# The first block's attention by pairs of heads, layer one's splits on GpSimd, and the weight stream in order of use

## The chip, the cores and the metric

The kernel is one program on one core of a Trainium2 chip. Its time is the device time of a run in microseconds; several runs are given by their median. A profiled execution shows the work of each engine: TensorE (PE, with its weight loads as PEld), VectorE (DVE), ScalarE (ACT), GpSimd (POOL) and SyncE (SP), which only issues the transfers of the weights.

## The reference

Two blocks of two layers each work on 256 tokens of width 1024 in float32. The change touches the first one, a latent transformer with a context of 256 further tokens. Of its layer:

```python
mod = silu_c @ w_ada[l] + b_ada[l]                    # adaLN: 6 x 1024 columns a layer, for latent and context
h = modulate(rms_norm(x, norm1_g[l]), sh1, sc1)       # h * (1 + scale) + shift
qa, ka, va, qb, kb, vb, ga, gb = split_in_proj(h @ w_in[l])
ya = window_attention_latent(rope(qa), rope(ka), va, kac, vac, sink_a[l])  # window of 128, a sink per head
yb = full_attention_latent(rope(qb), rope(kb), vb, kbc, vbc)
x = x + gt1 * merge_branches(ya, yb, ga, gb, w_proj_a[l], w_proj_b[l], w_out[l])
x = x + gt2 * swiglu(modulate(rms_norm(x, norm2_g[l]), sh2, sc2), w_ffn_gate[l], w_ffn_up[l], w_ffn_down[l])
```

Both attentions have 8 query heads of 64 dimensions on 2 key/value heads. In the first layer the context goes the same way (512 tokens in all; context queries see only the 256 context keys), in the second only the latent tokens are updated. The second block (sparse attention, stick-breaking attention, an mLSTM) isn't changed.

## The kernel before

**Weights.** All weights come as one stream of 504 slots of 512 KB (eight 128x128 blocks each), which SyncE loads in order into a ring of SLOTS = 7 buffers `raw`; the load of slot n waits until slot n - 7 is released. Every projection is float32 as three fp32r products: ScalarE rounds a slot to `high` (L1141), VectorE makes `low = raw - high` (L1507), and L745 to L747 multiply high by high, high by low, low by high. `high` and `low` have PAIRS = 4 buffers; a slot is released when its `low` is made. The slots of the adaLN weights are "plain": they are used from `raw` as they are (L826), 32 columns of the stationary side (silu(c)) at a time in column group k % 4, and released when used. A chunk of 512 adaLN columns is eight such products from four slots, then `adacopy` (VectorE, PSUM to SBUF), `adac` (TensorE, L838) and `mod` (VectorE).

**Order.** A planner (`Order`, `order_of_work`) writes one list of steps by hand, and every engine walks the same list and does its part of each step, in that order, with semaphores between them. `prepare` puts the `split` steps in as early as ring and buffers allow; `pool_share` says how many of them GpSimd takes in VectorE's place: (0, 1), none, up to the end of the first block. `o.hold` keeps splits out of the norms. `fill(n)` interleaves n blocks of waiting projections (`o.filling`) with a chain of small steps.

**Start.** adaLN chunks 0, 1 and 2, with the sums of squares of x and context between them, then mean, root (GpSimd's power, L1458) and broadcast (L867), then chunk 3, and then `gs` (scale factors) and the norm's eight tiles: L1625 scales, ScalarE adds the shift (high part), L1646 makes the low part. All four chunks must be there before the first tile. The constant tables (960 and 704 KB) are asked for on ScalarE's queue behind x and context.

**Layer.** Keys (2 slots), values (2 slots), in layer one adaLN chunks 4 and 5, queries (8 slots), the head norms of the second branch with fills of 3 + 3 blocks, then the attention. Its fill is, in layer one, chunks 6 and 7 and then gate tile and chunk in turn (16 gate tiles G of eight blocks, chunks 8 to 23), in layer two the 16 gate tiles alone (half as wide). Before, a unit is one head h, one branch b (0: window and sink, 1: full) and 128 queries t; layer one has 64 units, half of them with 512 keys and half with 256, layer two 32 with 512 keys. An iteration is: scores of unit i (L904), four fill blocks, transposes of unit i - 2 (L915), values of unit i - 3 (L928). VectorE adds the window (L1683), takes the maximum (L1685) and the sink (L1690); ScalarE takes the exponential with its sum (L1261); the turned probabilities are copied by ScalarE (L1271), each fourth by VectorE (L1700). After eight units `finish` divides by the sums (L1719) and `deliver` transposes the output (L941) and copies it over the queries (L1285). The score banks are 2, 3, 4, the transposes' 5 and 6, the values collect in bank 7.

Of the kernel before, what the change touches and what calls it, by code (L numbers as in the profile page):

```python
# [6 lines left out]
P = 128  # L7
# [18 lines left out]
ADA_EARLY = 4  # L26

# [45 lines left out]
class Order:  # L73
# [3 lines left out]
    def __init__(self, plain, total):  # L77
        self.plain, self.total = plain, total
# [4 lines left out]
        self.pool_share, self.hold = (0, 1), False  # L83
        self.sweeps, self.left_at, self.block_of, self.sweep_of = 0, {}, {}, {}
        self.ada_slots, self.uncollected = {}, []
# [19 lines left out]
    def prepare(self):  # L105
        if self.hold:
            return
        while self.next_split < self.total:
            n = self.next_split
            if n not in self.plain:  # L110
# [8 lines left out]
                self.step("split", n)  # L119
                self.released.add(n)  # L120
# [5 lines left out]
    def use(self, slot):  # L126
        if slot not in self.split_no:
            self.hold = False
            self.prepare()
# [44 lines left out]
    def ada(self, c):  # L174
        for k in range(KT):
            self.ada_slots[self.at // BLK] = 4 * c + k // 2 + 1
# [20 lines left out]
def order_of_work(plain, total):  # L197
    o = Order(plain, total)
# [29 lines left out]
    def first(l):  # L228
        last = l == N_LAYERS - 1
        n = SEQ if last else ALLT  # L230
        o.pool_share = (0, 1)
# [38 lines left out]
        units = [(b, t, h) for t in range(n // P) for b in range(2) for h in range(NH)]  # L270
        per = 4
        pending = []
        for i in range(len(units) + 4):
            if i < len(units):
                o.step("S", l, i, *units[i])
            o.fill(per)
            if pending and i % 8 == 5:
                o.step("deliver", l, *pending.pop(0))
            if 2 <= i < len(units) + 2:
                o.step("turn", l, i - 2, *units[i - 2])  # L280
            if 3 <= i < len(units) + 3:
                b, t, h = units[i - 3]
                o.step("PV", l, i - 3, b, t, h)
                if h == NH - 1:
                    o.step("finish", l, b, t)
                    pending.append((b, t))
        while pending:
            o.step("deliver", l, *pending.pop(0))
# [137 lines left out]
    for chunk, tiles in enumerate((range(0, 2), range(2, 5), range(5, 8))):  # L426
        o.run(o.ada(chunk))
        for k in tiles:
# [1694 lines left out]
```

## Time and profile before

| | us |
|---|---|
| median of 3 runs | 2274.36 (2271.99 to 2285.28) |
| profiled execution | 2274.49 |
| its span, first to last instruction | 2273.0 |
| TensorE busy | 2064.7 (91%) |
| VectorE busy | 1133.1 (50%) |
| ScalarE busy | 876.5 (39%) |
| GpSimd busy | 37.2 (2%) |
| mean granted TensorE clock | 0.944 |

Busy time is the union of an engine's instructions; the ends of matmuls are modelled, so that a start-to-start distance tells more than a duration. A float32 product (L904, L928, L826, L838) leaves two records, an fp32r product and a transpose one. Times in a timeline are from the span's start. Layer one of the first block runs from about 54 to 958 us (its attention from 193 to 464), layer two up to about 1412 (attention from 1037 to 1159), the second block behind it.

### The profile page before, as it was taken

To read this page: it belongs to the slowest core of one execution; us is meant where nothing else is said; L and a number is where in the kernel's file an instruction comes from. 1 tells how busy PE (TensorE), PEld (TensorE's weight loads), DVE (VectorE), ACT (ScalarE), POOL (GpSimd) and SP (SyncE) were. 2 spreads that over 40 slices of the span, in tenths; PEclk is the share of its full clock that TensorE was granted. 3 is DMA by queue.
4 is the path that set the end of the run, shared out by engine and by line. 5 is a ranking of instruction groups with operands and counts; after the bars stand their busy time and mean duration, and the time that the engine had idled before them with its cause. 6 is when DMAs were issued, how large, how long until landed. Compare 5 with 4: busy or idle time off the path is not lost.

```text
span 2273.0 us, 30554 instructions
## 1 busy us (share of the span) xinstructions
PE 2064.7 (91%) x12588; PEld 1714.5 (75%) x12588; DVE 1133.1 (50%) x1976; ACT 876.5 (39%) x1488; POOL 37.2 (2%) x37
## 2 busy tenths in 40 slices
PE   4899999998999999899988998898997889899886
PEld 1665666676788888687778998877787888778786
DVE  2334333364433333545455655568445756764555
ACT  2212333442321222333454444455452544644442
POOL 0000000000000000000000000000000000000100
PEclk7899999989999999899998999899998989999998
DMA  8223335522222222132123564433332444232231
GB/s 315 115 91 122 139 139 186 189 89 75 83 93 86 99 94 84 64 130 75 66 75 131 191 199 173 141 123 106 117 112 76 138 139 157 85 130 105 95 110 54
DMA packets 76554, 272.26 MB, mean 120 GB/s; under 512 B 8192, under 2 KB 11392, under 8 KB 76416
## 3 DMA queue, kind: packets, MB, share of 16 engines
q1 hardware_dynamic: 72576, 264.27, 33.4%
q10 hardware_dynamic: 3840, 6.04, 0.7%
q8 instruction: 100, 1.64, 0.3%
q14 instruction: 38, 0.31, 0.0%
HBM read 269.23 MB, written 1.05 MB: 119 GB/s over the span
## 4 chain that ended last, share of the span: by engine, by line
PE 73%; DVE 14%; ACT 6%; issue 3%; DMA 2%; POOL 1%; ACTq 0%; DVEq 0%; POOLq 0%
PE bank L745 19%; PE bank L747 18%; PE bank L746 18%; DVE low L1507 4%; PE bank L904 4%; PE bank L928 3%; ACT high L1141 3%; PE bank L915 2%; PE bank L826 2%; PE bank L867 1%; DMA xc<-ctx_in 1%; PE bank L893 1%; PE bank L838 1%; POOL few L1458 1%; DVE tmp L1625 1%
## 5 line engine op out<-in xcount | busy, mean ns | idle before, releaser
L745 PE MATMUL bank<-h,high 128*128 128x256 f32 (+1 forms) x2432 | 809.8, 333 | 54.1 <-issue 10.5
L746 PE MATMUL bank<-h,high 128*128 128x256 f32 (+1 forms) x2432 | 769.0, 316 | 0.0
L747 PE MATMUL bank<-h,low 128*128 128x256 f32 (+1 forms) x2432 | 769.0, 316 | 0.0
L1507 DVE TENSOR_TENSOR low<-raw,high 128x1024 fp32r<-128x1024 f32 x408 | 496.7, 1224 | 500.8 <-ACT high L1141 500.4
L745 PEld LDWEIGHTS bank<-h,high 128*128 128x128 f32 x2432 | 474.0, 195 | 154.5 <-issue 60.9
L746 PEld LDWEIGHTS bank<-h,high 128*128 128x128 f32 x2432 | 475.2, 195 | 29.8 <-issue 2.4
L747 PEld LDWEIGHTS bank<-h,low 128*128 128x128 f32 x2432 | 474.4, 195 | 30.0
L1141 ACT ACTIVATE high<-raw 128x1024 fp32r<-128x1024 f32 x408 | 426.5, 1050 | 127.0 <-PE bank L747 107.2
L1261 ACT ACTIVATE prob<-bank,small 128x512 f32<-128x512 f32 (+1 forms) x96 | 59.2, 616 | 195.9 <-DVE small L1690 111.5
L745 PE MATMUL bank<-hid,high 128*128 128x512 f32 (+1 forms) x352 | 118.2, 336 | 0.0
L746 PE MATMUL bank<-hid,high 128*128 128x512 f32 (+1 forms) x352 | 118.2, 336 | 0.0
L747 PE MATMUL bank<-hid,low 128*128 128x512 f32 (+1 forms) x352 | 118.2, 336 | 0.0
L904 PE MATMUL bank<-K,Q 64*128 64x512 f32 (+1 forms) x192 | 94.6, 573 | 0.0
L1685 DVE TENSOR_REDUCE small<-bank 128x1 f32<-128x512 f32 (+1 forms) x96 | 57.6, 600 | 63.0 <-PE bank L904 61.9
L928 PE MATMUL bank<-V,probT 128*128 128x64 f32 x640 | 83.7, 271 | 0.3 <-ACT probT L1271 0.3
L928 PEld LDWEIGHTS bank<-V,probT 128*128 128x128 f32 x640 | 80.6, 195 | 0.8 <-ACT probT L1271 0.5
L1528 DVE SCALAR_TENSOR_TENSOR xc<-bank,mod,xc 128x256 f32<-128x256 f32 x72 | 32.6, 480 | 95.9 <-PE bank L747 95.6
L1310 ACT ACTIVATE hid<-gt 128x512 fp32r<-128x512 f32 (+1 forms) x44 | 23.1, 525 | 145.2 <-DVE gt L1534 145.2
L1227 ACT ACTIVATE sq<-xc 128x256 f32<-128x256 f32 (+1 forms) x56 | 27.6, 496 | 127.0 <-DVE xc L1528 97.0
L826 PE MATMUL bank<-raw,silu_c 128*32 128x512 f32 x384 | 64.3, 644 | 9.9 <-ACT silu_c L1128 5.3
L746 PEld LDWEIGHTS bank<-hid,high 128*128 128x128 f32 x352 | 66.1, 188 | 8.0
L747 PEld LDWEIGHTS bank<-hid,low 128*128 128x128 f32 x352 | 66.1, 188 | 8.0
(261 smaller groups left out, 2418.9 us busy)
## 6 DMA issues: line engine op xcount, KB each, us to landing
raw<-stream SPq DMA_DIRECT2D x504, 512.0 KB, 3.3
xc<-x_in ACTq DMA_DIRECT2D x1, 1024.0 KB, 16.9
xc<-ctx_in ACTq DMA_DIRECT2D x1, 1024.0 KB, 28.4
out<-xc ACTq DMA_DIRECT2D x1, 1024.0 KB, 4.8
cst<-consts ACTq DMA_DIRECT2D x1, 960.0 KB, 28.8
cst<-consts ACTq DMA_DIRECT2D x1, 704.0 KB, 22.5
ukw<-uk ACTq DMA_DIRECT2D x1, 512.0 KB, 3.2
uvw<-uv ACTq DMA_DIRECT2D x1, 512.0 KB, 4.2
```

What stands on the lines that cost most here:

```text
L745: mm(dst, wh, xh, start=start, stop=False)
L746: mm(dst, wh, xl, start=False, stop=False)
L747: return mm(dst, wl, xh, start=False, stop=stop)
L826: ins = mm(banks[b][g, :], silu_c[:, k, :], raw[:, block // BLK % SLOTS, at:at + 512], start=k < 4, stop=k >= 4)
L904: mm(banks[b][:, 0:w], Q[l][half, 4 * b_ + h % 4, t * P:(t + 1) * P], K[l][half, b_, keys], start=True, stop=True).then_inc(S["S"], 1)
L915: ins = nc.tensor.transpose(banks[b][:, s * P:(s + 1) * P], prob[l][i % 3][:, s * P:(s + 1) * P], ident)
L928: ins = mm(banks[7][:, head(h)], probT[l][i % 2][:, s * P:(s + 1) * P], V[l][:, first + s, c:c + HD], start=s == 0, stop=s == w // P - 1)
L1141: do(high[:, i % PAIRS, :], raw[:, slot % SLOTS, :], ACTF.Copy).then_inc(S["hi"], 1)
L1261: do(prob[l][i % 3][:, 0:w], banks[bank_of[step]][:, 0:w], ACTF.Exp, bias=st[:, h:h + 1], accum_out=st[:, 8 + h:9 + h]).then_inc(S["exp"], 1)
L1507: tt(low[:, i % PAIRS, :], raw[:, slot % SLOTS, :], high[:, i % PAIRS, :].bitcast(F32), ALU.subtract).then_inc(S["lo_dve"], 1)
L1528: ins = stt(out=xc[:, jj, c], in0=ps[:, c], scalar=mod[:, at, s:s + 1], in1=xc[:, jj, c], op0=ALU.mult, op1=ALU.add)
L1685: nc.vector.tensor_reduce(st[:, h:h + 1], ps[:, 0:w], AX.X, ALU.max, negate=True).then_inc(S["masked_max"], 1)
```

## The change

- **Pairs.** A step now handles heads j and j + 4 of a branch, which lie in the two halves of the partitions of one query tile: two score products into two banks, two softmaxes, eight transposes into banks 5 and 6, both heads' values.
- **Order in an iteration.** Scores of pair i; 3 fill blocks; transposes of pair i - 1, copied by ScalarE (first head) and VectorE (second head) ahead of the exponentials of pair i; the new step `even`, in which VectorE divides the probabilities by their sum (sinks added) before they are turned; 3 fill blocks; values of pair i - LAG (1 in layer one, 2 in layer two); 2 fill blocks in layer one, 1 in layer two.
- **Values.** V is now the stationary side (64 columns) and the turned probabilities stream (128 columns); the output comes out turned and is copied from bank 7 over the queries (two copies each on ScalarE and VectorE). The transposes L941 and `finish` are gone.
- **GpSimd** makes `low` for all slots up to the end of layer one; from layer two on it is VectorE as before.
- **Start.** All sums of squares first, adaLN chunk 2, mean, chunk 3, broadcast, `gs` (which needs only 2 and 3), then chunks 0 and 1, then the norm. Its tiles 0, 3 and 6 let one split step in each. Of the constants only the identity (64 KB) comes at the start; the rest is asked for on ScalarE's queue at the norm's tile 2.
- **Stream.** A draft walk of the order finds which slot each use wants; SyncE loads `stream[source[n]]`.

```diff
 Order.__init__
-        self.pool_share, self.hold = (0, 1), False
+        self.pool_share, self.hold = (1, 1), False
...
+    def take(self, chunk=None, k=0):
+        if self.draft and self.at % BLK == 0 and self.at // BLK == len(self.source):
+            self.source.append(next(self.stream_split) if chunk is None else self.stream_plain[4 * chunk + k // 2])
...
 norm_tiles
+            if k % 3 == 0 and m == ("n1", 0):
+                o.prepare(1)
...
 first
-        o.pool_share = (0, 1)
+        o.pool_share = (1, 1) if n == ALLT else (0, 1)
...
-        for i in range(len(units) + 4):
-            if i < len(units):
-                o.step("S", l, i, *units[i])
-            o.fill(per)
...
+        pairs = [(b, t, j) for t in range(n // P) for b in range(2) for j in range(4)]
+        lag = LAG[l]
+        for i in range(len(pairs) + lag):
+            if i < len(pairs):
+                o.step("S", l, i, *pairs[i])
+            o.fill(3)
+            if 1 <= i <= len(pairs):
+                o.step("turn", l, i - 1, *pairs[i - 1])
+            if i < len(pairs):
+                o.step("exp", l, i, *pairs[i])
+                o.step("even", l, i, *pairs[i])
+            o.fill(3)
+            if i >= lag:
+                b, t, j = pairs[i - lag]
+                o.step("PV", l, i - lag, b, t, j)
+                if j == 3:
+                    o.step("deliver", l, b, t)
+            o.fill(2 if l == 0 else 1)
...
 start
+    for k in range(KT):
+        norm_sums(first_norm, k)
+    o.run(o.ada(2))
     o.step("sqsum", first_norm, KT - 1)
     o.step("mean", first_norm)
+    o.run(o.ada(3))
     o.step("bcast", first_norm)
     o.collect()
     o.step("gs", 0, 0)
+    o.run(chain(o.ada(0), o.ada(1)))
+    o.collect()
...
 TensorE, scores
+                    for g, b in enumerate(bank_of[step]):
+                        if b in freed:
+                            pe.wait_ge(*freed[b])
+                        mm(banks[b][:, 0:w], Q[l][head(g), 4 * b_ + j, t * P:(t + 1) * P], K[l][head(g), b_, keys],
+                           start=True, stop=True).then_inc(S["S"], 1)
+                        freed[b] = ("exp", 2 * no[step] - 1 + g)
...
 TensorE, values
+                    pe.wait_ge("turned_act", no[step])
+                    pe.wait_ge("turned_dve", no[step])
                     for s in range(w // P):
+                        for g in range(2):
+                            c = P * b_ + HD * g
+                            ins = mm(banks[7][head(g), j * P:(j + 1) * P], V[l][:, first + s, c:c + HD],
+                                     probT[l][2 * (i % LAG[l]) + g][:, s * P:(s + 1) * P], start=s == 0, stop=s == w // P - 1)
...
 ScalarE, exp
+                    for g, b in enumerate(bank_of["S", l, i, b_, t, j]):
+                        if b_ == 0:
+                            act.wait_ge("sink_max", sinks[l, i])
+                        do(prob[l][2 * (i % 2) + g][:, 0:w], banks[b][:, 0:w], ACTF.Exp, bias=st[:, g:g + 1],
+                           accum_out=st[:, 2 + g:3 + g]).then_inc(S["exp"], 1)
...
 ScalarE, norm
+                    if step == ("norm", ("n1", 0), 2):
+                        nc.scalar.dma_start(cst[:, :], consts).then_inc(S["in_cst"], 16)
+                        nc.scalar.dma_start(cst2[:, P:], consts2[:, P:]).then_inc(S["in_cst2"], 16)
...
 VectorE, even
+                    dve.wait_ge("exp", at + 1)
+                    if b_ == 0:
+                        dve.wait_ge("sunk_exp", sinks[l, i])
+                        tt(st[:, 2:4], st[:, 2:4], st[:, 4:6], ALU.add).then_inc(S["dve_own"], 1)
+                    nc.vector.reciprocal(st[:, 6:8], st[:, 2:4]).then_inc(S["dve_own"], 1)
+                    for g in range(2):
+                        p = prob[l][2 * (i % 2) + g][:, 0:w]
+                        ts(p, p, st[:, 6 + g:7 + g], None, ALU.mult).then_inc(S["even"], 1)
...
 SyncE
-                nc.sync.dma_start(raw[:, n % SLOTS, :], stream[n]).then_inc(S[f"slot{n % SLOTS}"], 16)
+                nc.sync.dma_start(raw[:, n % SLOTS, :], stream[work.source[n]]).then_inc(S[f"slot{n % SLOTS}"], 16)
```

## Rows read from the trace of the kernel before

**Rows 1.** Table by stretch: length, busy us and instructions by engine, PE clock, DMA, GB/s
```profile
193.00:454.00 261.00, 258.14 (x1451) 173.68 (x1451) 94.63 (x203) 90.90 (x214) 0.00 (x0) 0.99 0.44 161
...
600.00:700.00 100.00, 100.00 (x430) 80.57 (x429) 34.49 (x36) 28.16 (x36) 0.00 (x0) 1.00 0.27 95
```

**Rows 2.** TensorE's timeline, 512-key unit, layer one: start us, us, engine, line
```profile
226.42 1.12 PE L904 MATMUL bank<-K,Q 64*128 64x512 f32 x2
227.47 1.07 PE L826 MATMUL bank<-raw,silu_c 128*32 128x512 f32 x8
228.47 0.66 PE L915 MATMUL bank<-cst,prob 128*128 128x128 f32 x4
228.96 1.00 PE L928 MATMUL bank<-V,probT 128*128 128x64 f32 x8
229.89 1.12 PE L904 MATMUL bank<-K,Q 64*128 64x512 f32 x2
```

**Rows 3.** TensorE's timeline, part of a 256-key unit, layer one
```profile
431.48 0.56 PE L928 MATMUL bank<-V,probT 128*128 128x64 f32 x4
431.96 0.70 PE L904 MATMUL bank<-K,Q 64*128 64x256 f32 x2
432.59 1.06 PE L826 MATMUL bank<-raw,silu_c 128*32 128x512 f32 x8
```

**Rows 4.** TensorE's timeline, second block, products of two heads
```profile
1513.54 0.71 PE L980 MATMUL bank<-dqs,x 64*128 64x256 f32 x4
1514.08 0.40 PE L981 MATMUL bank<-dqs,x 64*128 64x128 f32 x4
1514.40 0.38 PE L745 MATMUL bank<-h,high 128*128 128x256 f32 x1
...
1532.26 0.40 PE L1004 MATMUL bank<-prob,SV 128*64 128x128 f32 x4
```

**Rows 5.** Groups by line, 193 to 425 us, TensorE: xcount | busy us, mean ns
```profile
L941 PE MATMUL bank<-cst,tmp 128*128 128x128 f32 x24 | 3.9, 286 | 0.0
```

**Rows 6.** Chain that ended last: start us, us, what; three adaLN products
```profile
158.58 1.01 PE bank L826 x6
```

**Rows 7.** Timelines of GpSimd and of VectorE, where both work, second block
```profile
1693.77 2.38 POOL L1466 TENSOR_TENSOR z<-z,dqs 128x1024 f32<-128x1024 f32 x1
1693.79 3.44 DVE L1866 TENSOR_TENSOR z<-z,dqs 128x1024 f32<-128x1024 f32 x1 [6.95 <-ACT dqs L1397]
```

**Rows 8.** Groups by line and form, 1037 to 1158 us (layer two's attention), VectorE
```profile
L1685 DVE TENSOR_REDUCE small<-bank 128x1 f32<-128x512 f32 x32 | 22.1, 689 | 17.0 <-PE bank L904 16.5
L1507 DVE TENSOR_TENSOR low<-raw,high 128x1024 fp32r<-128x1024 f32 x13 | 15.9, 1225 | 27.8 <-ACT high L1141 27.8
...
L1683 DVE TENSOR_TENSOR bank<-bank,cst 128x128 f32<-128x128 f32 x16 | 4.7, 295 | 9.8 <-PE bank L904 9.6
...
L1690 DVE TENSOR_TENSOR small<-small,small_sink 128x1 f32<-128x1 f32 x16 | 2.5, 159 | 0.5
```

**Rows 9.** Groups by form, 1500 to 2110 us, VectorE: scaling of 256 probabilities
```profile
L1849 DVE TENSOR_SCALAR prob<-prob,stats 128x256 f32<-128x256 f32 x16 | 5.6, 347 | 0.0
```

**Rows 10.** TensorE's timeline, layer two: the scores of two successive units
```profile
1093.22 1.12 PE L904 MATMUL bank<-K,Q 64*128 64x512 f32 x2
...
1097.12 1.12 PE L904 MATMUL bank<-K,Q 64*128 64x512 f32 x2
```

**Rows 11.** Groups by line and form, 1037 to 1158 us, ScalarE
```profile
L1261 ACT ACTIVATE prob<-bank,small 128x512 f32<-128x512 f32 x32 | 22.0, 688 | 60.8 <-DVE small L1690 34.4 <-DVE small L1685 26.3
...
L1141 ACT ACTIVATE high<-raw 128x1024 fp32r<-128x1024 f32 x13 | 13.7, 1053 | 0.0
```

**Rows 12.** Chain that ended last, in order of time, first 100 us
```profile
1.85 28.36 DMA xc<-ctx_in
...
53.83 0.88 DVE tmp L1625 x2
...
99.50 1.84 PE bank L838 x8
```

More of the change, by code:

```diff
@@ L73, with __init__ @@
 class Order:
[L77 to L78 removed]
+    def __init__(self, plain, total, source=None):
+        self.stream_plain, self.total = sorted(plain), total
+        self.stream_split = iter(n for n in range(total) if n not in plain)
+        self.draft, self.source = source is None, source or []
+        self.plain = {n for n, s in enumerate(self.source) if s in plain}
         self.steps, self.filling = [], []
@@ L103, in reload, with prepare @@
             self.loaded += 1
-    def prepare(self):
-        if self.hold:
+    def prepare(self, most=None):
+        if self.hold and not most or self.draft:
             return
-        while self.next_split < self.total:
+        while self.next_split < self.total and most != 0:
             n = self.next_split
@@ L119, in prepare @@
                 self.step("split", n)
+                most = most and most - 1
                 self.released.add(n)
@@ L501, in psum_banks @@
             bank[s[:2]] = turn("acc")
-        elif kind in ("S", "score", "latent", "read", "centre"):
+        elif kind == "S":
+            bank[s] = (turn("lgt"), turn("lgt"))
+        elif kind == "turn":
+            bank[s] = (turn("trp"), turn("trp"))
+        elif kind in ("score", "latent", "read", "centre"):
             bank[s] = turn("lgt")
@@ new lines, in vector_program @@
+                    (_, w), st, at = keys_of(t), stat(l, i), 2 * no[step] - 1
+                    for g, b in enumerate(bank_of[step]):
+                        ps = banks[b]
+                        dve.wait_ge("S", at + g)
+                        if b_ == 0 and t < 2:
+                            o = slice((1 - t) * P, (2 - t) * P)
+                            own += 1
+                            tt(ps[:, o], ps[:, o], const("window", t * P, t * P + P), ALU.add).then_inc(S["dve_own"], 1)
+                            dve.wait_ge("dve_own", own)
+                        if no[step] > 4:
+                            dve.wait_ge("even", at + g - 8)
+                        nc.vector.tensor_reduce(st[:, g:g + 1], ps[:, 0:w], AX.X, ALU.max,
+                                                negate=True).then_inc(S["masked_max"], 1)
@@ new lines, in vector_program @@
+                    dve.wait_ge("turn", 2 * no[step])
+                    if i >= LAG[l]:
+                        dve.wait_ge("PV", 2 * no[step] - 2 * LAG[l])
+                    nc.vector.tensor_copy(probT[l][2 * (i % LAG[l]) + 1][:, 0:w], banks[bank_of[step][1]][:, 0:w]).then_inc(S["turned_dve"], 1)
+                elif kind == "deliver":
+                    l, b_, t = key
+                    dve.wait_ge("PV", 8 * no[step])
+                    for odd in range(2):
+                        src, dst = out_of(l, b_, t, 1, odd)
+                        ins = nc.vector.tensor_copy(dst, src)
+                    ins.then_inc(S["delivered_dve"], 1)
```

257 lines of the change are left out of this document (98 added, 159 removed).

## The prediction

> **What bounds the kernel now.** I first read the table of stretches for the first block. Over layer one's attention TensorE works 258.14 of 261 us at a granted 0.99, VectorE 94.63 and ScalarE 90.90; in a plain stretch behind it TensorE works all 100 us, at 430 products in 100 us, so 0.233 us for a 512-column product and 5.6 us for a weight slot of 24 [rows 1]. The reader is to see that the first block is bound by TensorE's own work: what leaves its queue shortens the run, and work on the other engines costs nothing until it is late. Then I read the timeline of a unit (one head, 128 queries). With 512 keys it spends 1.05 us on the scores (L904), 0.49 on four transposes (L915) and 0.93 on the values (L928), 2.47 in all, beside 1.00 for four adaLN products (L826) [rows 2]. With 256 keys scores take 0.63 and values 0.48 [rows 3].
>
> **Scores and values by pairs.** The pair's score products use rows 0 to 63 and 64 to 127 of TensorE and different banks. No row shows that for L904, but the second block's L980/L981 is the same shape: two heads, each a 256-column and a 128-column product, are through in 0.86 us (1513.54 to 1514.40) [rows 4], where one 256-column product alone takes 0.63 [rows 3]; one after another they would need some 1.7. So two heads run side by side at the price of one. The values now hold V (64 columns) and stream 128 queries, the heads in the two halves of the columns: in L1004 four such records start at 1532.26 and take 0.40 [rows 4], of which I read about 0.11 per pair of records plus a tail (estimate). Bounds: the full gain, or none, where the two run in turn. I take the full gain, as both shapes stand in the trace. Rule: the Trainium skill, TensorEngine Tiling (Array Packing), Key Properties, says that tiles execute in parallel but that a change of tiling mode drains the engine; the rows agree with the first half, and the sum below holds its own price for changes.
>
> At 512 keys a pair has so far 2 x (1.05 + 0.49 + 0.93) = 4.94. After: scores 1.07, eight transposes 0.93 (0.16 for the first, 0.11 for each further one, as the 0.49 divides), values 8 x 0.11 + 0.2 = 1.07, together 3.07: 1.87 less. At 256 keys: 2 x (0.63 + 0.48) = 2.22 becomes 0.65 + 0.60 = 1.25: 0.97 less. Layer one has 16 pairs of each kind: 29.9 + 15.5 = 45.4 us less. The transposes of the output (L941, 24 in 3.9 us, 0.16 each [rows 5]) go: 8 x 4 x 0.16 = 5.2.
>
> **What the new fill costs.** Four adaLN products lie on four groups of 32 columns; six records, that is three products, take 1.01 us [rows 6], as long as four [rows 2]. A chunk of eight was filled 4 + 4, and is now filled 3 + 3 + 2: three groups for two. The head norms consume three sets of eight blocks before, so that each iteration holds one chunk or one gate tile: 16 chunks x 1.0 = 16 us more. One more change of shape per iteration: 32 x 0.1 = 3 (estimate from the 0.2 us between L928's last start and L904, against 0.11 in the stream of L928). Net on TensorE in layer one: 45.4 + 5.2 - 16 - 3 = 31.6 less.
>
> **GpSimd's splits.** A 128x1024 tensor-tensor takes GpSimd 2.38 us. The VectorE operation that began beside it took 3.44 [rows 7], where the same size takes 1.22 by itself [rows 8]: it ended about 1.1 after GpSimd did, so it stood still until then. Rule: the Trainium skill, SBUF — State Buffer, SBUF: two separate sides, calls the shared pair an exclusive lock which the loser of a two-input operation waits out; the row agrees. So in layer one each VectorE operation with two SBUF inputs may wait up to 2.38. In plain stretches a split has 5.6 us per slot and four slots of lead: hidden. In the attention the split of the next gate tile (ScalarE 1.05 [rows 11], then GpSimd 2.38) runs from about 1.8 to 4.2 us of an adaLN iteration; the sink operations of the first branch (two SBUF inputs) would start at 3.2 and now wait until 4.2; VectorE's copy of the transposes is queued behind them and ends at 5.35, while TensorE wants it at 4.1: 1.25 us in four iterations (two query tiles of 512 keys, two each): 5 us. With 256 keys the sinks come before GpSimd starts. Layer one: 31.6 - 5 = 27 us less.
>
> **Layer two** has only 512-key pairs, no adaLN, and splits still on VectorE: 16 x 1.87 + 16 x 0.16 - 1.6 = 31 less for TensorE. But the starts of two units lie 3.90 us apart [rows 10], 2.47 of it attention, so four blocks are 1.4 and an iteration with seven fills would be 3.07 + 0.1 + 2.45 = 5.6 us. Now the softmax is a loop over VectorE and ScalarE. For the first branch: window and maximum twice, 2 x (0.30 + 0.69 + 0.05) = 2.1 [rows 8]; sinks twice 0.16 and a start, 0.4; the copy of the turned probabilities lies beside ScalarE's two exponentials, 2 x 0.8 (0.69 [rows 11] and 0.1 for the read of the sum, an estimate); then add, reciprocal and two scalings of 512 columns (not in the trace at that width; 0.35 at 256 [rows 9]; between that and the 0.69 of a maximum, I take 0.45), 1.4: 5.8 us from maximum to maximum, and a split of 1.22 in it on most iterations: 6.6. The second branch has no windows and sinks and stays at 5.7. The mean is 6.15 against 5.6, over 15 iterations 8 us; the last pairs have no fills left and wait for the chain, 3 us more. 31 - 11 = 20 less.
>
> **The start.** The context lands at 30.2 us [rows 12] because it shares the DMA engines with the weights. TensorE now takes only chunk 2 before the mean, so 11 slots rather than 19 are asked for by then, and the constants (1.6 MB) come later: it should land at 23. But chunks 0 and 1 stand before the first norm tile on VectorE's queue (their copies, behind 8 more slots), so the first tile, 23.6 us after the context before (53.83 [rows 12]), comes 27 after it: at 50.3, 3.5 earlier. The eight tiles then meet three GpSimd splits: each second step (L1646, two SBUF inputs) can wait, and two DMA issues stand on ScalarE's queue between tiles, with VectorE and then TensorE behind: 5.5 later. Two us are lost. Behind V, four VectorE splits each wait for a transfer and stand before the copies of chunks 4 and 5, so that L838 comes at 99.50 [rows 12]; on GpSimd they block nothing: the queries start 5 us earlier. Bounds of the start: 8 less (no blocking) to 5 more. I take 2.5 less. The merge waits 1 us for blocked subtractions. The reordered stream moves no byte less; the order of use before was the stream's order, and chunks 2 and 3 first is all that changes.
>
> **Sum.** 27 + 20 + 2.5 - 1 = 48.5 less. The profiled execution took 2274.49 us, 0.1 above the median of the three; 2274.5 - 48.5 = 2226.
>
> **Rivals.** (1) *The chain decides.* The pair's softmax, two maxima, two exponentials and two scalings in series, is late in layer one too, where VectorE also copies the adaLN sums, and the scalings cost 0.69. For it: in 512-key pairs only about 1 us is free. Against it: VectorE works 94.63 of 261 [rows 1]. Half the gain in both attentions goes: 2249. (2) *No side by side.* If the wait between the two score products, or the alternation of the two value products, makes them run in turn, 1.92 per 512-key pair and 0.98 per 256-key pair come back: 32 x 1.92 + 16 x 0.98 = 77, of which layer two hides 12 in its loop: 2226 + 65 = 2291, slower by 0.7%; rows 4 speak against it. (3) *GpSimd sets the pace, the slower side.* In layer one's plain stretches some 100 slots are split by GpSimd. If a split waits for VectorE as VectorE waits for it, 2.38 + 3.44 = 5.8 is above the 5.6 us of a slot, from where the four slots of lead run out; at 6.5 a slot it costs 100 x 0.9 = 90: 2316, slower by 1.8%. Against it: VectorE has one or two such operations per slot, mostly 0.7 us. (4) *More than forecast.* No blocking, scalings at 0.35 and layer two bound by TensorE: 5 + 8 + 5: 2208.
>
> **How the numbers follow.** The forecast has 0.55, within 2214 to 2238; (1) 0.2, (2) 0.07, (3) 0.08, (4) 0.1. The range reaches to (4) and past (1): 2204 to 2260. A measurement of this kernel tells about 1% (23 us) from no change, so faster is below 2251.6: 0.55 + 0.1 and over half of (1), 0.75; slower is (3) and the far end of (2), 0.1; the rest, 0.15, is within 1%.
>
> **What would show it.** Right: pairs of L904's successor start some 14 ns apart and the pair is over in 1.1 us; the layer-one attention is about 27 us shorter and TensorE still works over 95% of it; the one of layer two shows TensorE waiting for the scaled probabilities or the maxima, and is 20 shorter; adaLN products come in groups of six, six and four records, about 1 us each; a VectorE operation beside a GpSimd split lasts 2 to 3.4 us. Wrong: score pairs of 2.1 us (rival 2), TensorE waiting for low on GpSimd in the feed-forward stretches (rival 3), waits before the transposes in layer one (rival 1).

## The result and the profile after

The changed kernel takes 2221.87 us (median; 2219.93 to 2227.03) beside 2277.34 us for the kernel before on the same chip: a ratio of 0.9759, with a 95% interval of 0.9735 to 0.9783. It is 2.4% faster. The forecast was 2226, worked out from a kernel before of 2274.5; by medians on one chip 55 us were saved. The profiled executions last 2273.0 and 2219.1 us, and 54 us lie between them.

The lines of the changed kernel have moved: scores are L930 (before L904), transposes L943 (L915), values L961 (L928), adaLN products L852 (L826), the gathering of a chunk L864 (L838), weight products L771 to L773 (L745 to L747), GpSimd's split L1472, VectorE's L1530, ScalarE's rounding L1162. I cut both executions at the same four events: the first score pair of layer one, the first `h` after its attention (ScalarE's L1315, before L1292), and the same two of layer two. The table of stretches between them, first of the kernel after, then of the kernel before (columns as in [rows 1]: stretch, length, busy us and instructions of TensorE, its weight loads, VectorE, ScalarE, GpSimd, then the granted clock):

```profile
188.30:433.60 245.30, 234.21 (x1455) 141.05 (x1454) 122.09 (x309) 87.06 (x227) 43.23 (x19) 0.98 0.50 178
433.60:1010.40 576.80, 547.00 (x2504) 440.43 (x2504) 163.60 (x290) 174.27 (x245) 199.47 (x87) 0.97 0.26 88
1010.40:1105.80 95.40, 91.49 (x761) 71.34 (x760) 75.02 (x162) 52.42 (x124) 0.00 (x0) 1.00 0.23 78
1105.80:2219.00 1113.20, 986.43 (x7124) 906.01 (x7124) 665.74 (x1166) 512.26 (x840) 19.80 (x19) 0.93 0.37 125
```

```profile
193.10:463.00 269.90, 266.01 (x1486) 180.67 (x1486) 96.73 (x207) 93.45 (x222) 0.00 (x0) 0.97 0.44 162
463.00:1037.60 574.60, 544.26 (x2504) 440.04 (x2504) 249.64 (x370) 175.65 (x246) 7.68 (x7) 0.97 0.26 88
1037.60:1158.90 121.30, 119.39 (x777) 91.82 (x776) 54.78 (x102) 55.51 (x120) 0.00 (x0) 0.99 0.18 61
1158.90:2273.00 1114.10, 988.46 (x7124) 907.06 (x7124) 665.99 (x1166) 512.39 (x841) 19.80 (x19) 0.93 0.37 125
```

The reader is to see three things. The two attentions give 24.6 and 25.9 us, the stretch before them 4.8 (193.1 to 188.3), the stretch between them loses 2.2, and the one behind them gains 0.9: 54.0 in all. In layer one TensorE's busy time fell by 31.8 us, but it now stands idle 11.1 us instead of 3.9. In layer two it fell by 27.9, with 3.9 us idle instead of 1.9.

TensorE's timeline of a 512-key pair in layer one after the change (start us, us, engine, line; x counts records, two to a product of this precision), to be held beside [rows 2]:

```profile
226.44 1.13 PE L930 MATMUL bank<-K,Q 64*128 64x512 f32 x4
227.50 1.06 PE L852 MATMUL bank<-raw,silu_c 128*32 128x512 f32 x6
228.49 0.66 PE L943 MATMUL bank<-cst,prob 128*128 128x128 f32 x4
228.98 0.60 PE L943 MATMUL bank<-cst,tmp 128*128 128x128 f32 x4
229.51 1.06 PE L852 MATMUL bank<-raw,silu_c 128*32 128x512 f32 x6
230.50 1.09 PE L961 MATMUL bank<-probT,V 128*64 128x128 f32 x16
231.53 1.05 PE L852 MATMUL bank<-raw,silu_c 128*32 128x512 f32 x4
232.51 1.13 PE L930 MATMUL bank<-K,Q 64*128 64x512 f32 x4
```

By the distances of starts, the scores of both heads take 1.06 us (one head took 1.05), the transposes 1.02 and the values 1.03. The adaLN groups of six, six and four records take 0.99, 0.99 and 0.98 us.

Where TensorE waits in layer one's attention, by the waits of the kernel after (waited for: us, times, longest):

```profile
PE bank L930 <- ACT prob L1287: 4.3, 1, 4.3
PE bank L961 <- DVE probT L1745: 4.0, 5, 0.9
PE bank L943 <- DVE mod L1594: 2.6, 1, 2.6
```

These are the first softmax, the copies of the turned probabilities, and a wait that is put down to `mod` and has its cause in GpSimd's splits, as the part on the prediction shows.

### The profile page after: what moved, and what is told of

Same layout as the page of the kernel before. It is cut to its first block, busy times and chain, and to the rows that moved or that the text cites. A ratio compares the mean times of both kernels' runs of the same rounds, so it can differ in the third digit from the quotient of the medians.

```text
span 2219.1 us, 30747 instructions
## 1 busy us (share of the span) xinstructions
PE 2004.4 (90%) x12540; PEld 1656.4 (75%) x12540; DVE 1085.8 (49%) x2044; ACT 863.9 (39%) x1494; POOL 305.6 (14%) x149
## 3 DMA queue, kind: packets, MB, share of 16 engines
HBM read 269.23 MB, written 1.05 MB: 122 GB/s over the span
## 4 chain that ended last, share of the span: by engine, by line
PE 71%; DVE 15%; ACT 7%; issue 4%; POOL 1%; DMA 1%; ACTq 0%; DVEq 0%
PE bank L771 20%; PE bank L773 18%; PE bank L772 18%; DVE low L1530 4%; ACT high L1162 3%; PE bank L852 2%; PE bank L930 2%; PE bank L961 2%; PE bank L943 1%; PE bank L893 1%; DVE h L1671 1%; PE bank L864 1%; POOL few L1481 1%; PE bank L919 1%; DVE tmp L1648 1%
## 5 line engine op out<-in xcount | busy, mean ns | idle before, releaser
L771 PE MATMUL bank<-h,high 128*128 128x256 f32 (+1 forms) x2432 | 815.5, 335 | 59.9 <-issue 13.7
L773 PE MATMUL bank<-h,low 128*128 128x256 f32 (+1 forms) x2432 | 771.0, 317 | 0.0
L771 PEld LDWEIGHTS bank<-h,high 128*128 128x128 f32 x2432 | 477.1, 196 | 147.3 <-issue 56.8
L773 PEld LDWEIGHTS bank<-h,low 128*128 128x128 f32 x2432 | 477.0, 196 | 30.8
L1530 DVE TENSOR_TENSOR low<-raw,high 128x1024 fp32r<-128x1024 f32 x296 | 360.1, 1223 | 268.3 <-ACT high L1162 267.3
L1162 ACT ACTIVATE high<-raw 128x1024 fp32r<-128x1024 f32 x408 | 426.5, 1050 | 128.6 <-PE bank L773 117.7
L1472 POOL TENSOR_TENSOR low<-raw,high 128x1024 fp32r<-128x1024 f32 x112 | 268.5, 2402 | 559.6 <-ACT high L1162 559.6
L1481 POOL TENSOR_TENSOR few<-few,halves 128x2 f32<-128x2 f32 (+2 forms) x28 | 27.3, 976 | 886.2 <-DVE few L1622 886.2
L1557 DVE TENSOR_TENSOR gt<-bank,gt 128x512 f32<-128x512 f32 (+1 forms) x44 | 24.6, 558 | 200.4 <-PE bank L773 197.6
L773 PE MATMUL bank<-hid,low 128*128 128x512 f32 (+1 forms) x352 | 117.9, 335 | 0.0
L771 PE MATMUL bank<-hid,high 128*128 128x512 f32 (+1 forms) x352 | 117.9, 335 | 0.0
L852 PE MATMUL bank<-raw,silu_c 128*32 128x512 f32 x384 | 75.6, 671 | 14.5 <-ACT silu_c L1152 13.7
L773 PEld LDWEIGHTS bank<-hid,low 128*128 128x128 f32 x352 | 66.0, 187 | 8.2
L772 PEld LDWEIGHTS bank<-hid,high 128*128 128x128 f32 x352 | 66.0, 187 | 8.2
L771 PEld LDWEIGHTS bank<-hid,high 128*128 128x128 f32 x352 | 66.0, 187 | 8.1
```

The source lines that it names most:

```text
L771: mm(dst, wh, xh, start=start, stop=False)
L772: mm(dst, wh, xl, start=False, stop=False)
L773: return mm(dst, wl, xh, start=False, stop=stop)
L852: ins = mm(banks[b][g, :], silu_c[:, k, :], raw[:, block // BLK % SLOTS, at:at + 512], start=k < 4, stop=k >= 4)
L1162: do(high[:, i % PAIRS, :], raw[:, slot % SLOTS, :], ACTF.Copy).then_inc(S["hi"], 1)
L1472: tt(low[:, i % PAIRS, :], raw[:, slot % SLOTS, :], high[:, i % PAIRS, :].bitcast(F32), ALU.subtract).then_inc(S["lo_pool"], 1)
```

## The experiments

Each ratio is to the kernel before on the same chip; the changed kernel's is 0.9759. "Attention one" and "attention two" are the lengths of the two stretches cut as above: 269.9 and 121.3 us before, 245.3 and 95.4 after. Stretches that two kernels share still differ between executions: the first score pair of nominally equal starts came at 186.8 to 191.4 us, attention one lasts 245.3 to 246.8 and attention two 95.0 to 96.1 where nothing in them was changed, but the stretch behind attention two, the same in all changed kernels but one, lasts 1107.8 to 1117.6. So an edit is read from its own attention, and a difference of 2 or 3 us in the whole is not read. The runs were also made on several chips, where the kernel before takes 2274.4 to 2277.3 us; where medians and ratios give different distances between two changed kernels, both are named.

### One product pair on the same rows

```diff
-mm(banks[b][:, 0:w], Q[l][head(g), 4 * b_ + j, ...], K[l][head(g), b_, keys], ...)
+mm(banks[b][:, 0:w], Q[l][head(0), 4 * b_ + j, ...], K[l][head(0), b_, keys], ...)
```

> The changed kernel with both score products of a pair on the same half of the array: the second takes the first head's rows of queries and keys again, so the second head's scores (and the output) are those of the first; the work, its size and every wait are the same, only the side-by-side run is gone. Theory A (two 64-row products run at once only on different rows): a 512-key score pair costs 2.1 us instead of 1.06, a 256-key pair 1.2 instead of 0.6: 32 x 1.05 + 16 x 0.55 = 42 us more, 2264, nearly all on the path. Theory B (the gain came from closer issue, not from the array's halves): 2222 within 5. Theory C (part is absorbed in waits for the softmax): 2240.

2254.27 us, ratio 0.9899 (0.9883 to 0.9916); attention one 268.5, attention two 105.8. TensorE's timeline of this run:

```profile
271.05 1.98 PE L930 MATMUL bank<-K,Q 64*128 64x512 f32 x4
272.96 1.05 PE L864 MATMUL bank<-vec,ada_part 128*128 128x2 f32 x8
```

The pair takes 1.91 us instead of 1.06. So the two halves of the array really work at once, and that alone is worth 32 us (attention one is 23.2 longer, attention two 10.4). Successive starts of pairs are 0.85 us further apart with 512 keys and 0.43 with 256; I had expected 1.05 and 0.55. The sum of these is 16 x 0.85 + 16 x 0.43 + 16 x 0.84 = 34.

### Values head by head

```diff
-for s in range(w // P):
-    for g in range(2):
+for g in range(2):
+    for s in range(w // P):
```

> The changed kernel with the value products of a pair ordered head by head (four key tiles of one head, then four of the other) instead of alternating heads; same products, same results. Theory A (side by side needs neighbours on different column halves): a pair of 8 products costs 1.9 instead of about 1.1 us with 512 keys, 1.0 instead of 0.6 with 256: 32 x 0.8 + 16 x 0.4 = 32 us more, 2254. Theory B (the halves overlap whatever the order): 2222 within 3.

2232.00 us, ratio 0.9801 (0.9782 to 0.9820); attention one 253.7, attention two 102.6. The values of a 512-key pair:

```profile
1046.43 1.58 PE L961 MATMUL bank<-probT,V 128*64 128x128 f32 x16
```

This is 0.49 us more than the 1.09 of the alternating order. With 256 keys the distances of pairs are unchanged (8.55 and 4.77 us, against 8.54 and 4.77). Each theory was half right: alternation matters with eight products and not with four. Why is open. Head by head the values still cost 1.51 us by starts, where two heads took 2 x 0.93 before [rows 2]; so of the gain in values the smaller part, up to 0.35 us, is the new shape, and the larger, 0.49, is the alternation. The two attentions are 8.4 and 7.2 us longer, 16 pairs of 0.49 each. The whole run is only 10 longer; in the profiled execution the two other stretches are 3.9 shorter, which is within their spread.

### Order of copies and exponentials

The two exponentials and the scaling of pair i come ahead of the transposes of pair i - 1 and their copies:

```diff
+if i < len(pairs):
+    o.step("exp", l, i, *pairs[i])
+    o.step("even", l, i, *pairs[i])
 if 1 <= i <= len(pairs):
     o.step("turn", l, i - 1, *pairs[i - 1])
-if i < len(pairs):
-    o.step("exp", l, i, *pairs[i])
-    o.step("even", l, i, *pairs[i])
```

> The changed kernel with the order within a pair turned round: exponentials and the scaling of pair i first, then the transposes of pair i - 1 and their copies. Theory A (the copies are what the values wait for): in layer one the values come in the same turn, so their copies arrive about 2.5 us later and TensorE waits where it had 3 + 3 blocks to cover them: about 1.5 us in each of 32 pairs, +45, while layer two, whose values come one pair later, changes by under 0.3 us a pair, +5: 2270. Theory B (the fill covers it): 2222 within 5.

2270.79 us, ratio 0.9962 (0.9941 to 0.9984); attention one 293.9 (48.6 more), attention two 96.9 (1.5 more). TensorE's waits in attention one:

```profile
PE bank L961 <- DVE probT L1745: 36.0, 17, 3.8
```

Nearly the whole gain of the change goes with this one swap (its ten runs lie between 2256 and 2277 us). The first reason is the one expected, the values wait for the copies: 32 us more than in the changed kernel. The second was in no theory: TensorE's granted clock over attention one is 0.91 instead of 0.98, and the same products keep it busy for 253.6 us instead of 234.2, which makes 19 of the 48.6. So TensorE was idle more often, and then worked more slowly. Where the values come one pair later the swap costs nothing that can be told.

### Values one step behind in layer two as well

```diff
-LAG = (1, 2)
+LAG = (1, 1)
```

> The changed kernel with the values of layer two one step behind the scores, as in layer one, instead of two, and half of the buffers for the transposed weights. Theory A (in layer two no adaLN lies in the fills, and the values would wait for the copies): about 1.5 us in each of 16 pairs, +24: 2246. Theory B (three blocks of fill, 0.7 us each, cover the copies): 2222 within 3.

2232.84 us, ratio 0.9806 (0.9787 to 0.9824); attention two 106.7 (11.3 more). The waits in it:

```profile
PE bank L961 <- DVE probT L1745: 11.1, 9, 1.8
```

Theory A's mechanism at half its size: nine of the sixteen pairs wait, 1.2 us each.

### Every split on VectorE

```diff
-self.pool_share, self.hold = (1, 1), False
+self.pool_share, self.hold = (0, 1), False
-o.pool_share = (1, 1) if n == ALLT else (0, 1)
+o.pool_share = (0, 1)
```

> The changed kernel with every split of a weight tile on VectorE, as in the kernel before; nothing else differs. Theory A (GpSimd's splits cost by stalling VectorE, and VectorE has room): the first norm ends at about 60 us instead of 67 (three stalls of 2 to 6 us go, three splits of 0.69 us come), the groups of adaLN chunks 4 and 5 and the power behind GpSimd's queue lose nothing, attention of layer one loses its four stalls of 1 us: 2222 - 7 - 3 - 4 = about 2208. Theory B (VectorE is short of time in layer one's attention, GpSimd relieves it): 32 pairs take about 0.2 us more each, 2228, the start's 7 us included. Theory C (waits elsewhere take the place): 2222 within 3.

2235.95 us, ratio 0.9832 (0.9789 to 0.9875). I had expected a gain of 14 us and it is a loss of 14 by the medians (17 by the ratios); theory B had the sign and not the size. Attention one is 258.7, 13.4 longer. Its waits, and then VectorE's timeline around one of them:

```profile
PE bank L961 <- DVE probT L1745: 18.3, 17, 1.9
```

```profile
248.85 1.23 DVE L1530 TENSOR_TENSOR low<-raw,high 128x1024 fp32r<-128x1024 f32 x1 [3.68 <-ACT high L1162]
250.00 1.28 DVE L1712 TENSOR_REDUCE small<-bank 128x1 f32<-128x512 f32 x2
251.19 0.68 DVE L1745 COPY probT<-bank 128x512 f32<-128x512 f32 x1
```

The split, which itself waits for ScalarE's rounding, stands ahead of the maxima in VectorE's queue. The scores of this pair start at 247.17, so the maxima start 2.8 us behind them instead of 1.2, and the copy, queued behind the maxima, 4.0 instead of 3.2. The waits for the copy grew from 4.0 to 18.3 us; 3.7 us of other waits went, and TensorE was busy 2.7 us longer, at a granted 0.97 instead of 0.98. VectorE works half of the time here; it is late in one place of its queue.

### VectorE's splits up to chunk 5, GpSimd's from there

```diff
 o.run(chain(o.ada(4), o.ada(5)))
 o.collect()
+o.pool_share = (1, 1)
```

(together with the edit of the run above)

> The changed kernel with VectorE's splits until adaLN chunk 5 is done, GpSimd's from there to the end of layer one. If theory A holds and the start is where GpSimd costs: the start's part of the gain alone, 2222 - 9 = about 2213, and e1 stands 4 us below it (attention's stalls). Theory B: this one is the best of the two, 2213, with e1 at 2228. Theory C: 2222.

2225.50 us, ratio 0.9775 (0.9742 to 0.9808); attention one 246.2. None of the 9 us that I had expected of the start came. The start does not get better without GpSimd; the first score pair stands at 193.3 us, where the kernel before has it, against 188.3. TensorE's waits between 66 and 112 us say why:

```profile
PE bank L865 <- DVE ada_part L1590: 6.8, 2, 3.7
```

In the changed kernel the same wait is 0.9 us. VectorE's splits stand before the copies of chunks 4 and 5 again, as the prediction said of the kernel before. With three splits among its tiles the norm ends late in either case (a VectorE split there takes 1.23 and waits 1.13 for ScalarE's rounding).

### No splits among the tiles of the first norm

```diff
-if k % 3 == 0 and m == ("n1", 0):
-    o.prepare(1)
```

> The changed kernel without the three splits that it issues among the eight tiles of the first norm; they come after it, as before. Theory A (the splits hold the norm up, by GpSimd's lock here as by VectorE's own time in the run with VectorE's splits, and the early splits give nothing back): the norm's last tile at about 61 us instead of 67, the products of K start as the splits come, and K ends 3 to 5 us earlier: 2218. Theory B (what ends K's wait is the splits and not the norm): the norm ends at 61, but the splits then queue up, and K ends where it did or up to 4 us later: 2222 to 2226. Theory C (the norm's slowness is not the splits'): norm and K as in the changed kernel, 2222.

2219.88 us, ratio 0.9770 (0.9744 to 0.9796): no difference that can be told. The norm ends 8.3 us earlier (58.9 against 67.2), and K is drained at the same time within 0.6 us, because its slots are now split in one run behind the norm. ScalarE's rounding, GpSimd's splits, and K's first drain in this run:

```profile
57.91 3.88 ACT L1160 ACTIVATE high<-raw 128x1024 fp32r<-128x1024 f32 x4
59.03 9.38 POOL L1470 TENSOR_TENSOR low<-raw,high 128x1024 fp32r<-128x1024 f32 x4 [29.93 <-ACT high L1160]
68.99 0.60 ACT L1179 ACTIVATE K<-bank 128x512 f32<-128x512 f32 x1 [7.19 <-PE bank L771]
```

This is theory B: whichever of norm and splits goes first, the other is late.

### GpSimd's splits in the kernel before

```diff
-self.pool_share, self.hold = (0, 1), False
+self.pool_share, self.hold = (1, 1), False
...
-o.pool_share = (0, 1)
+o.pool_share = (1, 1) if n == ALLT else (0, 1)
```

> The kernel before with one part of the change alone: its splits up to the end of layer one on GpSimd. Theory A (stalls cost, VectorE had room): the first norm up to 6 us later by three or more stalls, adaLN 4 and 5 by 3, softmax units of layer one stalled but partly covered, +5: 2277 + 10 = about 2287. Theory B (VectorE relieved of 0.69 us every 3.9 us gains): 2277 - 5 = 2272. Theory C: 2277 within 3.

2272.27 us, ratio 0.9980 (0.9962 to 0.9998); attention one 264.1 against 269.9. What is worth 14 us in the changed kernel is worth some 2 to 5 in the old one. There the values stand a unit behind the transposes, so that a late copy has more time; that this is the reason was not tested.

### GpSimd's splits everywhere

```diff
-o.pool_share = (1, 1) if n == ALLT else (0, 1)
+o.pool_share = (1, 1)
```

> The changed kernel with GpSimd's splits in the first layers of both blocks' attention and everything behind them, not up to the end of layer one only. Theory A (GpSimd's split pays where VectorE's copies are late, which in layer two they are not; elsewhere its 2.4 us in place of 1.2 and its stalls of VectorE's two-input operations cost): layer two's attention unchanged within 2 us, the norms and head norms of layer two and the second block later by 5 to 15 in all: 2232. Theory B (VectorE is short of time all over): faster, 2215. Theory C: 2222 within 3.

2270.40 us, ratio 0.9983 (0.9968 to 0.9998): 48 us slower than the changed kernel, in the expected direction but more than twice my 10. Attention two accounts for 6 of it, the second block for most of the rest. In the second half of the run, from the end of layer two's attention, TensorE's waits for `few` (the roots of the norms, which GpSimd's power and VectorE make) are 39.1 us instead of 18.3 and those for VectorE's `prob` 13.8 instead of 3.9. How much of this is VectorE stopped by a split, and how much is GpSimd itself late with a power or a `low`, no run takes apart. In attention two VectorE's timeline shows the stall, and GpSimd's the cause:

```profile
1031.38 1.85 DVE L1719 TENSOR_TENSOR small<-small,small_sink 128x2 f32<-128x2 f32 x1
```

```profile
1030.84 2.37 POOL L1472 TENSOR_TENSOR low<-raw,high 128x1024 fp32r<-128x1024 f32 x1 [4.33 <-ACT high L1162]
```

### Fills of 4, 4 and 0

In layer one; layer two keeps 3, 3 and 1:

```diff
-o.fill(3)
+o.fill(3 if last else 4)
...
-o.fill(3)
+o.fill(3 if last else 4)
...
-o.fill(2 if l == 0 else 1)
+if last:
+    o.fill(1)
```

> The changed kernel with layer one's fills as 4, 4 and 0 blocks around a pair instead of 3, 3 and 2, so that adaLN's eight quarter-array products stand as two groups of four again, as before. Theory A (a group costs about 1.0 us whether it holds four products, three or two): one group fewer in each of the 16 pairs that meet a chunk, 2222 - 16 = about 2207, and the adaLN pair's period of about 7 us goes to about 6. Theory B (the third fill covers the copies of the transposes, which now stand bare): the values wait for their copies by about 1 us in each of 32 pairs, 2222 - 16 + 32 = about 2238. Theory C: the two are equal, 2222.

2205.66 us, ratio 0.9690 (0.9656 to 0.9724); attention one 230.1, so 15.2 less. TensorE's timeline of the same kind of pair as above:

```profile
227.55 1.13 PE L931 MATMUL bank<-K,Q 64*128 64x512 f32 x4
228.61 1.07 PE L853 MATMUL bank<-raw,silu_c 128*32 128x512 f32 x8
...
230.63 1.06 PE L853 MATMUL bank<-raw,silu_c 128*32 128x512 f32 x8
...
232.65 1.13 PE L931 MATMUL bank<-K,Q 64*128 64x512 f32 x4
```

The pair takes 5.10 us instead of 6.07: one group of adaLN products is gone. Nothing took its place: the waits for the copies are 4.3 us, where they were 4.0.

### Eight blocks ahead of the first pair

The last edit, and chunk 8 filled ahead of the first scores of layer one:

```diff
 lag = LAG[l]
+if not last:
+    o.fill(8)
```

> Fills of 4, 4 and 0 in layer one, and besides eight blocks (adaLN chunk 8) ahead of the first score pair of layer one, so that the first pairs lie beside gate products rather than beside the short adaLN ones. Theory A (in the changed kernel TensorE stands 4.3 us in the second pair, waiting for the first exponentials, and then runs at a granted clock of 0.55 to 0.59 for about 8 us): the wait is covered and the clock stays up: against the run with fills of 4, 4 and 0 alone (2206) 4 us of wait less and about 3 of clock, 2 us more ahead: -5, 2201. Theory B (the first exponentials come later by the 2 us and the wait only moves): 2206 within 3.

2200.53 us, ratio 0.9679 (0.9658 to 0.9701). By the medians this is 5 us below the last run, as expected, but by the ratios only 2.5, and their intervals overlap, so that the gain in the whole is near what can't be told. The traces show it in one place: attention one is 222.3; it begins 2.2 us later and is 7.8 shorter. Some of this goes again, for the stretch behind it is 4.0 longer (578.9 against 574.9). The granted clock over the last 10 us of attention one and the first 10 behind it is 0.51 and 0.64, in the last run 0.56 and 0.76; the blocks that moved ahead are now missing there, but that this is the cause was not tested. The stretches of four us at its head, first of the changed kernel, then of this one:

```profile
192.00:196.00 4.00, 0.34 (x1) 0.00 (x0) 2.40 (x7) 1.50 (x2) 0.00 (x0) 1.00 0.98 387
196.00:200.00 4.00, 3.38 (x9) 1.88 (x9) 2.44 (x8) 1.32 (x5) 0.00 (x0) 0.55 0.62 252
200.00:204.00 4.00, 4.00 (x14) 3.23 (x14) 1.56 (x5) 0.00 (x0) 0.00 (x0) 0.59 0.00 0
```

```profile
192.00:196.00 4.00, 4.00 (x28) 2.19 (x21) 3.76 (x7) 0.00 (x0) 0.00 (x0) 1.00 0.63 186
196.00:200.00 4.00, 4.00 (x18) 3.20 (x17) 2.02 (x7) 2.58 (x5) 0.00 (x0) 1.00 0.84 317
```

In the changed kernel TensorE works 0.34 of 4 us while the first softmax is under way, and the granted clock then stands at 0.55 and 0.59 for 8 us. With gate products beside the first pair it neither waits there nor loses its clock. This is the fastest kernel of the study, 21 us below the changed one (18 by the ratios).

### The same with every split on VectorE

```diff
-self.pool_share, self.hold = (1, 1), False
+self.pool_share, self.hold = (0, 1), False
...
-o.pool_share = (1, 1) if n == ALLT else (0, 1)
+o.pool_share = (0, 1)
```

> The run with fills of 4, 4 and 0 and eight blocks ahead, with every split on VectorE instead of GpSimd's up to the end of layer one. Theory A (what GpSimd is worth is the lateness of VectorE's copies before the values; it grows as TensorE's work around them shrinks): in the adaLN pairs, which take 5.1 to 5.3 us instead of 6.1 to 7.1, the copies come still later: against the run with GpSimd's splits (2200.5) the 14 us of the like comparison in the changed kernel plus up to 1 us in each of 16 pairs, 2222. Theory B (its worth is fixed, a split is a split): +14, 2214. Theory C (the 4 + 4 blocks ahead of the values leave time enough): under +8, 2206.

2216.44 us, ratio 0.9723 (0.9699 to 0.9746): above the last run by 16 us by the medians and by 10 by the ratios. Attention one is 235.2, which is 12.9 longer, with 17.1 us of waiting for `probT` in 16 waits instead of 6.0. In the first comparison it was 13.4 longer: the worth did not grow, and theory B fits best.

## Why the prediction was right

Total: 48.5 us less were forecast, and the profiled executions show 54.0. The forecast's own range (2214 to 2238) held the time. The single steps did less well than the sum. Layer two gave 5.9 us more than its 20 and the start 2.3 more than its 2.5, layer one 2.4 less than its 27, the stretch between 1.2 less, and 0.9 fell to a stretch with no forecast; that the sum is off by no more than 5.5 is in part luck.

**TensorE in layer one, 31.6 less: right.** Its busy time fell by 31.8. The 512-key scores were put at 1.07 and measured 1.06, the values at 1.07 and measured 1.03, the transposes at 0.93 and measured 1.02. Three adaLN groups of about 1.0 us for two stood as forecast, and the run with 4, 4 and 0 gave the 16 us back that the prediction had charged for them.

**GpSimd's splits in layer one, 5 us lost: wrong in its place and in what it was compared with.** The prediction said that the sinks (L1719) would be stopped by the split and hold up the copy. VectorE's line L1719 in attention one:

```profile
L1719 DVE TENSOR_TENSOR small<-small,small_sink x16: 161/161/959, 194.2 to 397.6; 128x2 f32<-128x2 f32 x16
```

The durations are the shortest, the median and the longest in ns: in at least half of the sixteen nothing stopped them, and the longest stall was 0.8 us. The split of 2.37 us begins in the adaLN pair at 228.16, beside maxima and copies, which read from a bank. The idle time did grow by 7 us, but 4.3 us of waits are the first softmax, of which 1.28 are a table load on ScalarE (`ACT_TABLE_LOAD` at 194.49). The 2.6 us that the waits put down to `mod` are GpSimd's, by another operation: the scaling of the probabilities (L1737), whose inputs are one SBUF tile and a factor for each row. At the end of the attention VectorE's and then GpSimd's timeline read:

```profile
421.92 4.91 DVE L1737 TENSOR_SCALAR prob<-prob,small 128x256 f32<-128x256 f32 x2
426.75 0.74 DVE L1712 TENSOR_REDUCE small<-bank 128x1 f32<-128x256 f32 x2
```

```profile
419.63 9.39 POOL L1472 TENSOR_TENSOR low<-raw,high 128x1024 fp32r<-128x1024 f32 x4 [10.94 <-ACT high L1162]
```

Two scalings that otherwise take 0.34 each end at 424.5 and 426.8, 0.15 us behind the second and the third split, and `mod` and the transposes come behind them. The run with all splits on VectorE has no such wait. So a stall by GpSimd did cost TensorE about 3 us, near the 5 of the forecast, but at the end, where four splits follow one another, and not at the sinks. The larger mistake was what I compared with: I took VectorE's splits as free because VectorE works 94.63 of 261 us [rows 1]. In the new loop they would have cost 13 to 14 us (the run with all splits on VectorE), because the copies are queued behind them. That GpSimd's part is one of the gains was not in the prediction.

**TensorE in layer two, 31 less: 3 too much.** Busy time fell by 27.9. The distance of pairs is 5.81 us, put at 5.6; over 15 of them that is 3.

**The softmax loop in layer two, 8 us and 3 for the tail: this step failed.** The prediction put the first branch's loop at 6.6 us with a split and 5.8 without (its terms add up to 5.5), and wanted TensorE to wait for it. In the head of the attention, where VectorE never idles, its timeline gives the loop, from the window of one pair's first maximum to that of the next pair:

```profile
1023.96 0.29 DVE L1707 TENSOR_TENSOR bank<-bank,cst 128x128 f32<-128x128 f32 x1
...
1025.94 0.16 DVE L1719 TENSOR_TENSOR small<-small,small_sink 128x2 f32<-128x2 f32 x1
...
1026.21 1.22 DVE L1530 TENSOR_TENSOR low<-raw,high 128x1024 fp32r<-128x1024 f32 x1
1027.35 0.68 DVE L1745 COPY probT<-bank 128x512 f32<-128x512 f32 x1
1027.95 0.15 DVE L1730 TENSOR_TENSOR small<-small 128x2 f32<-128x2 f32 x1
...
1028.34 0.88 DVE L1737 TENSOR_SCALAR prob<-prob,small 128x512 f32<-128x512 f32 x2
1029.13 0.29 DVE L1707 TENSOR_TENSOR bank<-bank,cst 128x128 f32<-128x128 f32 x1
```

1023.96 to 1029.13 is 5.17 us, with the split in it. From 1026.21 to 1027.95 VectorE does the split and the copy in the time in which ScalarE takes the exponentials; I had 1.6 us for that and then 1.22 for the split behind it. The other terms were high by 0.1 to 0.2 each (maxima 1.98 for 2.1, sinks 0.27 for 0.4, the end 1.18 for 1.4). So the loop is shorter than TensorE's 5.81, and TensorE sets the pace: this part of rival 4 came true. The 11 us of loop and tail were 2 us of idle time in fact; with 3 us less from TensorE's own work, 20 forecast became 25.9.

**The start, 2.5 less: 4.8, by other sizes.** The context landed at 18.6 us (put at 23), and the first norm tile came at 45.75 (50.3, before 53.83 [rows 12]). The norm was put 5.5 us longer and took 7.5 more (45.75 to 67.2, before 53.83 to 67.8), and K ended where it had ended before: of the 8 us nothing was left and nothing more was lost, where the forecast had 3.5 us of gain turn into 2 of loss. The chain of the kernel after in the norm:

```profile
54.22 2.91 DVE h L1671 x2
...
61.43 5.80 DVE h L1671 x4
...
95.96 7.96 POOL low L1472 x3
103.92 1.61 POOL few L1481
```

L1671 has two SBUF inputs and takes 0.88 for two by itself; beside GpSimd's splits it took 2.9 and, for four, 5.8. The run without early splits shows that this stall costs nothing in the end. Behind V the queries' first products start 6.1 us earlier (96.2 against 102.3; forecast 5). Here GpSimd's queue holds one surprise, the power of the head norm, which waits behind three splits in a row; TensorE waits 2.2 us for it. It still stands 3.9 us earlier than before (103.9 against 107.8). No run takes the start's other parts by themselves, the order of the chunks, the later constants and the order of the stream, so what each is worth is not shown.

**The merge, 1 us lost:** 2.2 between the attentions, near what can't be told.

**The rivals.** (1), the chain decides, didn't come: TensorE was busy 95% of attention one. But the runs with the exponentials first (+49) and with a lag of one in layer two (+11) show how near it is. (2) was priced too high: breaking the pair's scores costs 32 us and setting values head by head 10, so the two would have given some 2264 and not 2291; the 1.92 us a pair were 0.85 and 0.49. (3) didn't come: 112 GpSimd splits take 2.40 us each, and the stretch between the attentions is 2.2 us longer in 577. Where slots are shorter, in the second block, GpSimd's splits do cost: 48 us in the run that keeps them to the end.

## What to carry to other kernels

A saved microsecond of a bounding engine is gained only where the next engine's queue is in the right order: ask of each operation that the bounding engine waits for (here the copies of the transposes) what stands before it in its queue, since an engine at half load can still be late there. Work in groups that cost the same for two, three or four members should be filled up before anything else is tuned; that edit alone gave 16 us. A loop's first turn has no work behind it, and a wait there is paid for a second time in TensorE's clock; long fill beside it avoided both here, though part of the gain was lost again behind the loop.

## What was unexpected in the hardware

- A GpSimd operation of 2.37 us stopped a VectorE operation of 128x2 elements, with two SBUF inputs, from 0.16 us up to a median of 1.69 and a longest of 2.37 us (L1719 in the run with GpSimd's splits everywhere), while the maxima, which read a bank, kept their 0.69. The Trainium skill, SBUF — State Buffer, SBUF: two separate sides, says that the shared pair is held for the whole instruction by whichever starts first and that the other fully blocks; the row agrees, down to a two-column operation that ends 0.02 us after GpSimd's.
- A scaling of one SBUF tile by a factor for each row (L1737, 128x256, 0.34 us by itself) was stopped too: two of them took 4.91 us beside a run of GpSimd's splits in the changed kernel.
- TensorE had 0.34 us of work in 4 us, and was then granted 0.55 and 0.59 of its clock for the next 8, near the lower of its two levels. Two records of L930 span 2.07 us there, where two of the same shape take 1.12 at the full clock [rows 2].
- Two heads' value products, eight of them, cost 0.49 us more head by head than in turn; four of them cost the same either way. The cause is open.
